# Turning the memory tokens by VectorE instead of TensorE, in a two-layer hybrid decoder kernel

## The reference, cut to what matters

```python
def rms_norm(x, g):
    return x * rsqrt(mean(x * x, axis=-1) + 1e-6) * g

mkv   = (rms_norm(mem, mem_norm_g) @ w_mem_kv).reshape(1, 256, 2, 4, 256)   # w_mem_kv: 2048 x 2048
mem_k = rms_norm(mkv[:, :, 0], mem_k_norm_g)
mem_v = mkv[:, :, 1]
h = x
h = h + even_layer(h, ..., mem_k, mem_v)  # DeltaNet, gated conv module, memory attention
h = h + odd_layer(h, ..., mem_k, mem_v)   # stick-breaking attention, memory attention
```

## Time and profile before

| what | value |
|---|---|
| median of three runs | 1333.56 us |
| the profiled execution's own time | 1333.2 us |
| its span, first to last instruction | 1331.5 us |
| VectorE busy | 972.8 us, 73% |
| ScalarE busy | 746.8 us, 56% |
| DMA queues' packets | 59% and 1% of 16 engines |
| granted TensorE clock | 1.000 |

### The profile page before, as it was taken

How to read it: one execution, slowest core, us unless ns; L and a number is a source line. 1 busy time by engine, 2 the same in 40 slices (tenths; PEclk the granted TensorE clock), 3 DMA queues, 4 the chain that set the end, 5 groups by cost and what they waited for, 6 DMA issues and landing times.

```text
span 1331.5 us, 18050 instructions
## 1 busy us (share of the span) xinstructions
PE 1324.3 (99%) x6733; PEld 1125.4 (85%) x6733; DVE 972.8 (73%) x1502; ACT 746.8 (56%) x1167; POOL 104.9 (8%) x104
## 2 busy tenths in 40 slices
PE   9999999999999999999999999999999999999998
PEld 9998899888888888888888888888888888888887
DVE  5557588898898998685656477688697787666663
ACT  6556633476435556586446446847747667764341
POOL 2000301003010100000001020020020100000000
PEclk9999999999999999999999999999999999999999
DMA  9655464555756995675455665465565565764652
GB/s 314 200 178 181 139 193 140 150 175 159 231 174 195 298 288 193 198 224 177 152 175 159 221 190 172 156 202 156 184 203 174 163 203 160 240 229 146 206 190 79
DMA packets 143153, 251.89 MB, mean 189 GB/s; under 512 B 14897, under 2 KB 27098, under 8 KB 143066
## 3 DMA queue, kind: packets, MB, share of 16 engines
q1 hardware_dynamic: 140345, 246.02, 59.0%
q10 hardware_dynamic: 2720, 4.72, 1.0%
HBM read 240.61 MB, written 10.09 MB: 188 GB/s over the span
## 4 chain that ended last, share of the span: by engine, by line
PE 79%; DVE 1%; POOL 0%; issue 0%; DVEq 0%
PE job L1820 48%; PE job L1830 24%; PE mixer L1841 2%; PE mixer L2033 1%; PE mixer L2053 1%; PE mixer L2062 1%; PE mixer L2075 1%; PE mixer L1950 0%; PE mixer L2061 0%; PE mixer L2076 0%; PE mixer L1930 0%; DVE cvr L1587 0%; DVE wlo L1339 0%; PE mixer L1963 0%; PE mixer L1938 0%
## 5 line engine op out<-in xcount | busy, mean ns | idle before, releaser
L1820 PE MATMUL job<-whi,xhi 128*128 128x512 f32 x1532 | 612.0, 399 | 0.0
L1820 PE MATMUL job<-whi,xlo 128*128 128x512 f32 x1532 | 597.5, 390 | 0.0
L1339 DVE TENSOR_TENSOR wlo<-raw,whi 128x1024 fp32r<-128x1024 f32 x431 | 524.4, 1237 | 66.7 <-ACT whi L991 65.5
L991 ACT ACTIVATE whi<-raw 128x1024 fp32r<-128x1024 f32 x431 | 445.5, 1056 | 183.5 <-PE job L1830 129.2
L1830 PE MATMUL job<-wlo,xhi 128*128 128x512 f32 x1532 | 410.1, 389 | 0.0
L1830 PEld LDWEIGHTS job<-wlo,xhi 128*128 128x128 f32 x1532 | 287.6, 188 | 60.7
L1820 PEld LDWEIGHTS job<-whi,xhi 128*128 128x128 f32 x1532 | 287.9, 188 | 57.9 <-DVE xlo L1390 0.5
L1820 PEld LDWEIGHTS job<-whi,xlo 128*128 128x128 f32 x1532 | 288.1, 188 | 57.2
L1587 DVE SCALAR_TENSOR_TENSOR cvr<-cvr,vt 128x255 f32<-128x255 f32 (+14 forms) x240 | 106.4, 502 | 0.2
L1817 PE MATMUL job<-xhi,whi 128*128 128x256 f32 x376 | 94.1, 288 | 0.0
L1817 PE MATMUL job<-xlo,whi 128*128 128x256 f32 x376 | 92.1, 283 | 0.0
(11 more groups left out here) (292 smaller groups left out, 993.2 us busy)
## 6 DMA issues: line engine op xcount, KB each, us to landing
raw<-in_od_w_in_dram SPq DMA_DIRECT2D x160, 512.0 KB, 4.4
raw<-in_ev_w_in_dram SPq DMA_DIRECT2D x143, 512.0 KB, 4.1
raw<-in_ev_w_out_dram SPq DMA_DIRECT2D x48, 512.0 KB, 5.4
raw<-in_od_w_out_dram SPq DMA_DIRECT2D x48, 512.0 KB, 5.1
raw<-in_w_mem_kv_dram SPq DMA_DIRECT2D x32, 512.0 KB, 4.9
proj<-turned_blocks SPq DMA_DIRECT2D x48, 128.0 KB, 4.4
turned_blocks<-proj SPq DMA_DIRECT2D x8, 512.0 KB, 5.4
reg<-in_mem_dram ACTq DMA_DIRECT2D x4, 512.0 KB, 5.3
```

Source lines behind the costliest of these rows:

```text
L991: act(whi[:, c % RING, :, :], raw[:, c % RAWS, :, :], ACT.Copy).then_inc(s_hi, 1)
L1339: vec.tensor_tensor(wlo[:, c % RING, :, :], raw[:, c % RAWS, :, :], whi[:, c % RING, :, :].bitcast(F32), ALU.subtract).then_inc(s_lo, 1)
L1820: mm(pj[j % 2][n][:, :], x[:, s, cols], h, start=first, stop=False)
```

## The change

`mem` is laid out so that 32 by 32 block turns, which VectorE can do, are all that is needed. Partitions 32b to 32b + 31 get the columns 512b to 512b + 511, of tokens a * 32 + j on partition 32b + j. One VectorE transpose `mt` p of 128 by 512 elements takes, of every run of 16 columns, columns 2p and 2p + 1. Its input is read with a step of 16 elements, and partition q of the result holds columns 16q + 2p and 16q + 2p + 1 for all 256 tokens: two fills. So fill 24 + k holds features k, 16 + k, 32 + k and so on, and the rows of `w_mem_kv` (2048 by 2048) are loaded in that order: partition q of chunk i of a job gets rows 16q + 2i and 16q + 2i + 1. The gains of the norm come in the same order by one small DMA more. `memt`, where the turned tiles go, has room for four fills and lies in `mix`, tiles 4 to 7. The two activations for the squares become eight of 512 columns, with sums that lie on four groups of 32 partitions; VectorE brings them together by 16 small copies and a sum. `xt` of `mem` has no TensorE step; `mt` 0 to 3 stand at positions 148, 150, 152, 154, `mt` 4 to 7 at 157, 159, 161, 163, each with .26 in the ledger.

```diff
-... "xt": .18, "mf": .16, "bas": .1}
+... "xt": .18, "mt": .26, "mf": .16, "bas": .1}
...
-        stream(5, CH0[J_MEM] - 11 + k, [(("xt", F_MEM + k), 0)])
-        stream(5, CH0[J_MEM] - 2 + k, [(("xt", F_MEM + 8 + k), 0)])
+        for half, start in ((0, CH0[J_MEM] - 11 + k), (8, CH0[J_MEM] - 2 + k)):
+            if k % 2 == 0:
+                stream(5, start - 1, [(("mt", (half + k) // 2), 0)])
+            stream(5, start, [(("xt", F_MEM + half + k), 0)])
...
-        memx = reg[:, :].rearrange("p (t d) -> p t d", t=T)
+        memx = reg[:, :].rearrange("p (a d) -> p a d", a=8)
+        memt = mflat[:, 4 * S:8 * S].rearrange("p (k s) -> p k s", k=4)
...
 def load_chunk(c):
+                if name == "mem":
+                    src = w[name][:, c0:c0 + 512].rearrange("(p k) n -> p k n", p=128)[:, 2 * (c - CH0[j]):2 * (c - CH0[j]) + 2, :]
...
+            sp.dma_start(mgain[:, :], vecs(vrow)[1][1].rearrange("k p -> (k p)").rearrange("(p k) -> p k", k=16)).then_inc(s_vrow, 16)
...
 # ScalarE, do_xt
+                if F_MEM <= n < F_OB:
+                    sc.wait_ge(s_vrow, 16 * 15)
+                    sc.wait_ge(s_jt, turn_count["mt", (n - F_MEM) // 2])
+                    fill_wait(n)
+                    act(xhi[:, SLOT[n], :], memt[:, n % 4, :], ACT.Copy, scale=xt_gain(n)).then_inc(s_xh, 1)
+                    return
...
 # ScalarE, do_rstd
+                if src == 1:
+                    for a in range(8):
+                        ins = act(pflat[:, 512 * (a % 4):512 * (a % 4) + 512], memx[:, a, :], ACT.Square, accum_out=msum[:, a:a + 1])
+                        if a == 3:
+                            link(ins)
...
 # ScalarE, do_mload
-                sc.dma_start(memx[:, :, 512 * b:512 * b + 512],
-                             mem[:, 512 * b:512 * b + 512].rearrange("(t p) d -> p t d", p=128)).then_inc(s_min, 16)
+                sc.dma_start(memx[32 * b:32 * b + 32], mem[:, 512 * b:512 * b + 512].rearrange("(a j) d -> j a d", j=32)
+                             ).then_inc(s_min, 16)
...
 # VectorE
+            def do_mt(p):
+                ve.wait_ge(s_min, 64)
+                ve.wait_ge(s_xl, F_OA + 8 if p < 2 else F_MEM + 2 * p - 2)
+                vec.transpose(memt[:, 2 * (p % 2):2 * (p % 2) + 2, :].rearrange("p k s -> p (k s)"),
+                              memx.rearrange("p a (i k) -> p k a i", k=16)[:, 2 * p:2 * p + 2]).then_inc(s_jt, 1)
...
 # VectorE, do_xt
+                    vec.scalar_tensor_tensor(out=xlo[:, SLOT[n], :], in0=memt[:, n % 4, :], scalar=xt_gain(n),
+                                             in1=xhi[:, SLOT[n], :].bitcast(F32), op0=ALU.mult, op1=ALU.subtract).then_inc(s_xl, 1)
...
 # VectorE, do_rstd
+                if src == 1:
+                    for a in range(4):
+                        for b in range(4):
+                            ins = vec.tensor_copy(mquar[32 * a:32 * a + 32, :, b], msum[32 * b:32 * b + 32, a:8:4])
+                    link(ins)
+                    link(vec.tensor_reduce(ssq[:, src, :], mquar[:, :, :], AX.X, ALU.add))
...
 # TensorE, do_xt
+                if F_MEM <= n < F_OB:
+                    return
```

More of the change, by code:

```diff
@@ L461, in prog, with blocks_turned @@
         tanhs = {0: slot(2), 1: slot(3), 4: tiles(20), 5: tiles(0), 10: slot(0), 11: slot(1)}
+        turn_no = {i: n for n, i in enumerate(i for st, i in plan if st == "lt")}
+        turn_count = {q: n + 1 for n, q in enumerate(q for q in plan if q[0] in ("lt", "mt"))}
         def exchanged(e, transfers=5):
-            return s_xg[e % 3], 80 * (e // 3) + 16 * transfers
+            return s_xg[turn_no[e] % 3], 80 * (turn_no[e] // 3) + 16 * transfers
+        def blocks_turned(e):
+            return s_jt, turn_count["lt", e]
         def landed(e):
@@ L635, in banks @@
             if step == "xt":
-                return [i % 3 if 8 <= i < F_OB else i % 4]
+                return [] if F_MEM <= i < F_OB else [i % 3 if 8 <= i < F_OA else i % 4]
             if step == "mao":
@@ L721, in xt_gain @@
         def xt_gain(n):
-            return (gain("ev_norm_g", n) if n < F_OA else gain("mem_norm_g", n - F_MEM) if n < F_OB
+            return (gain("ev_norm_g", n) if n < F_OA else mgain[:, n - F_MEM:n - F_MEM + 1] if n < F_OB
                     else gain("od_norm_g", n - F_H))
         def turned(n):
-            return n + 1 if n < F_OA else n - F_MEM + 17 if n < F_OB else n - F_H + 33
+            return n + 1 if n < F_OA else n - F_H + 17
         def mix_tile(n):
@@ L773, in load_chunk @@
                     sp.wait_ge(s_lo, c - RAWS + 1)
-                sp.dma_start(raw[:, c % RAWS, :, :], w[name][r:r + 256, c0:c0 + 512].rearrange("(k p) n -> p k n", p=128)
-                             ).then_inc(s_raw[c % RAWS], 16)
+                if name == "mem":
+                    src = w[name][:, c0:c0 + 512].rearrange("(p k) n -> p k n", p=128)[:, 2 * (c - CH0[j]):2 * (c - CH0[j]) + 2, :]
+                else:
+                    src = w[name][r:r + 256, c0:c0 + 512].rearrange("(k p) n -> p k n", p=128)
+                sp.dma_start(raw[:, c % RAWS, :, :], src).then_inc(s_raw[c % RAWS], 16)
             sp.dma_start(*vecs(vrow)[0]).then_inc(s_gain, 16)
@@ L823, in do_xw @@
             def do_xw(e):
[L824 to L827, removed]
+                sp.wait_ge(*blocks_turned(e))
+                if turn_no[e] >= 3:
+                    sp.wait_ge(s_xg[turn_no[e] % 3], 80 * (turn_no[e] // 3))
+                sp.dma_start(bass.AP(dram_x, 131072 * e, [[1024, 128], [1, 1024]]), stage[e]).then_inc(s_xg[turn_no[e] % 3], 16)
             def do_xr(e):
@@ L1049, in do_rstd @@
                     sc.wait_ge(s_scp, 4)
-                o = 0 if src == 1 else 2048
-                link(act(pflat[:, 0:2048], (memx if src == 1 else hid)[:, 0, :], ACT.Square, accum_out=ssq[:, src, 0:1]))
-                ins = act(pflat[:, o:o + 2048], (memx if src == 1 else hid)[:, 1, :], ACT.Square, accum_out=ssq[:, src, 1:2])
+                if src == 1:
[3 more added lines that the diff above has]
+                            link(ins)
+                    ins.then_inc(s_ss, 1)
+                    return
+                o = 2048
+                link(act(pflat[:, 0:2048], hid[:, 0, :], ACT.Square, accum_out=ssq[:, src, 0:1]))
+                ins = act(pflat[:, o:o + 2048], hid[:, 1, :], ACT.Square, accum_out=ssq[:, src, 1:2])
                 ins.then_inc(s_ss, 1)
@@ L1666, in do_lt @@
                     ve.wait_ge(s_mks, e - 5)
-                    ve.wait_ge(*((s_z, 16) if e == 6 else (s_xl, F_OA + 8)))
+                    ve.wait_ge(*((s_z, 16) if e == 6 else (s_xl, F_OB)))
                 elif e in (9, 10):
```

15 lines of the change are left out of this document (8 added, 7 removed).

## The result

The changed kernel takes 1340.93 us (median of 4 runs, 1338.13 to 1341.14) against 1333.22 of the kernel before on the same chip. The profiled execution took 1341.14, its span 1339.4.

A forecast was written before the change was run, and what follows sets the result against it. TensorE, busy 99%, was taken to bound the kernel: 4.1 us of transposes removed, less waits of 1.45 and 1.7 us (3.1 together), net -1.0, from 1333.56 to 1332.6 us; range 1329.3 to 1336.8.

The forecast's parts named there:

- TensorE's 0.256 us per pair: Each fill's pair of `mem` transposes costs TensorE this much; removing 16 pairs gains 4.1 us.
- both waits: New TensorE waits for VectorE's `xlo` at chunk 167, 1.45 us, and GpSimd's `lnacc` at 169, 1.7 us.
- The ledger's order: Eight entries of .26 move conv items later: item 123 from position 163 to 167, `lnm` from 165 to 169.
- VectorE's wait for the squares: At `rstd`, VectorE waits 4.4 us for ScalarE's eight squares, not 3.09 as before.
- The `w_mem_kv` loads at nothing: Weight loads whose neighbouring partitions read 128 KB apart, not 8 KB, were taken to cost nothing.
- The block turn: Each `mt` on VectorE takes 0.62 us from start to start, from a turn of as many elements at 0.71.
- The row nearest to it: Trace row with a 64-byte step on the writing side, 15 elements, 163 ns; taken as support for 0.62 us.
- the second rival: Strided read makes each block turn nearly twice as long: 3.2 us more, net +2.2, 1335.8 us; chance 0.17.
- The copies: 16 small copies on VectorE at `rstd`: 1.1 to 2.7 us, 1.2 taken.
- GpSimd's sums: GpSimd's two sums after conv item 123 take 2.60 us, making `lnacc` ready at 547.0.
- The second wait: TensorE, already delayed by 1.45 us, waits 1.7 us more for GpSimd's `lnacc` at `lnm`, ahead of chunk 169.
- 43 us of cover: Last `mem` load, issued at 440.24, is first needed at 488.75; no plausible landing exceeds that.

The follow-up runs named there:

- the version with both waits moved and the plain read: Changed kernel with the row sums at position 168, `lnm` at 170 and block turns reading 512 neighbouring elements: 1330.45 us, ratio 0.9977.
- the two profiles: Profiles of the changed kernel in its first measurement (1340.93 us) and when run again without edit (1339.04 us, ratio 1.0044).
- the 128-partition form: Changed kernel with the same layout of `mem`, loaded by eight DMAs of 128 partitions by 512 columns instead of four of 32 partitions: 1355.49 us.
- the plain-read version: Changed kernel with its eight block turns of `mem` reading 512 neighbouring elements instead of every 16th: 1337.63 us, ratio 1.0038.

## Why the prediction was wrong

**Right.** TensorE's 0.256 us per pair, as the steps between 149 and 160 show, and whole in the version with both waits moved and the plain read. The ledger's order: item 123 and `lnm` where it put them. The place and the owner of both waits, `xlo` at 167 and `lnacc` at 169. VectorE's wait for the squares, 4.4 forecast, 4.18 measured. The `w_mem_kv` loads at nothing. (TensorE's waits before are six, in five groups, not five; nothing hangs on it.)

**The block turn, 0.62 taken, 0.98 measured from start to start.** The row nearest to it, on writes of 15 elements, was no evidence on a read of 512: 15 elements at 0.7 ns more are 10 ns, too little to be seen in it. The six turns that the forecast counted are 2.2 us. It let turns 0 and 1 vanish in the wait before `zg` 5, but there is no such wait: VectorE comes to `zg` 5 without a pause, at 501.80 and 498.27 in the two profiles, so all eight count, 2.9 us. Taking the step out gives 3.2 us of the stage between the two profiles without a wait at 146 (5.4 to 2.2), and 1.4 or 3.3 of the medians. This was the second rival. Its place and sign were right, its price above the measured one (1.15), and its sum below the time, for the steps that follow.

**The copies, 1.2 taken, 2.8 measured.** They were priced by 128-partition operations at 0.07. These cross partition groups, and come each 0.17, the upper bound that the text gave. Within their groups they took 1.5. In medians it is worth 0.7 us, with intervals as wide.

**GpSimd's sums, 2.60 taken, 4.5 to 4.8 measured.** With the clock behind it, this step alone turns the sign: with VectorE's two prices as forecast the kernel is still 3.8 us slower. VectorE's prices alone would have turned it too: 2.2 and 1.6 us more in the forecast's sum make 1336.4. The 2.60 was measured beside a VectorE with gaps. The forecast filled the gaps, and kept the number. The second wait, 1.7 in the forecast, is 3.6 in the three profiles where TensorE came to it at the full clock, and 1.6 where the lower clock at 167 had held TensorE back already. That VectorE's work beside it is the cause rests on where the sums end, 0.6 us behind the last `rest` of an unbroken run in eleven profiles, behind an `xlo` from SBUF in a twelfth, and on their lengths (0.73 for one alone; for both 1.8 beside an `xlo` and a block turn, 2.5 to 2.6 beside one `rest`, 4.5 to 4.8 beside `rest` back to back), not on a run that changes this alone. The Trainium skill's page "GPSIMD Engine Reference", section "1. Specifications", has GpSimd share its SBUF interfaces with VectorE and contend with instructions of two SBUF inputs, which `rest` is; it gives no size. The rows agree.

**The clock, not in the sum.** Behind a new wait TensorE ran some 3.4 us at 1.2 GHz, about 1.7 us lost: twice in the changed kernel's first profile, once in its second. The forecast let a wait cost its own length; at 2.4 GHz it costs 0.3 more, and with the lower clock some 2 more.

**The wait at 160, not looked for.** The forecast held VectorE against chunks 167 and 169 only. VectorE's backlog shows first at the `evac` behind the copies, where TensorE waits 0.6 and 1.5 us. In the end this adds nothing, since VectorE runs without a pause from the copies to its last conv item, and TensorE waits for that: what it loses at 160 it doesn't lose later.

**The wait at 146, not in the sum.** 2.0 us and the clock's 1.6, in the first profile and not in the second. I gave the `mem` loads 43 us of cover and asked only whether they come in time for their own user. They did. They may have been late for somebody else, an exchange in a stage whose DMA share is 0.95. What is shown is the slower landing, the longer write where the wait came, and more slow executions of the kernel before with these loads. That the loads lengthen the write isn't shown: with the same loads it took 8.0 to 9.6 us in seven profiles, moving them made it worse, and the 128-partition form did not work. The cause of this wait stays open.

**The sum, closed for both profiles.** First: -4.1 of transposes, +0.7 before the stage, +3.6 at 146, +0.9 at 160 (wait 0.6), +4.2 at 167 and 168 (2.3 and the clock), +1.9 at 169: +7.2, against +7.27 at the last chunk. Second: -4.1, +0.2 before the stage, -0.3 at 146, +1.8 at 160 (wait 1.5), +2.7 at 167, +5.5 at 169 (3.6 and the clock): +5.8, against +5.59.

The second can be closed along the forecast's own steps too. It had `lnacc` ready at 547.0, and it was ready at 551.7. 2.2 of these 4.7 us are GpSimd's. 2.5 are VectorE's: the copies and the sum behind them 1.5, and the four turns that follow 1.4, less 0.4, since the squares ended that much sooner. TensorE then pays 0.3 to start again and 1.6 for the clock. -1.0 and 6.6 make +5.6.

**What the chances missed.** The rivals changed one price each. The waits are in series on one VectorE, so errors of one sign add: the turns 2.2, the copies 1.6, GpSimd 2.2, the clock 1.6. Both of VectorE's prices at the bounds that the text gave, 3.2 and 1.5 us over those taken, make 1332.6 + 4.7 = 1337.3, outside the range as given.

## What to carry to other kernels

Work moved from the engine that bounds the kernel to one 86% busy is paid where the second engine waits for something else: move such a wait behind the next deadline (here the row sums, worth 7 to 9 us), and give the new work its entry in the scheduler's ledger. A duration measured beside idle neighbours isn't the duration once you fill them; ask of each row what ran beside it. And ask of a load not only whether it is early enough for its own user, but what else travels beside it: here that question was left out, and part of the loss stayed unexplained.

## What the runs showed of the hardware

- A VectorE block turn of 128x512 takes 703 ns from neighbouring elements and 1064 ns at a read step of 64 bytes (the plain-read version, the changed kernel).
- Sixteen 32x2 copies take 2.8 us when they cross partition groups, 1.5 within them. One lasts 0.15 to 0.16 us in both cases; only those within a group overlap.
- A GpSimd addition of 128x256 takes 0.73 us alone and up to 3.9 beside VectorE's subtractions back to back; it ends 0.6 us after the last of them. VectorE pays too: sixteen copies beside two such additions took 3.8 us instead of 2.8.
- The granted clock fell to 1.2 GHz in or behind twelve TensorE waits of 2.04 to 9.5 us, in the changed kernel for 3.4 us each time, and not behind two of 2.29 and 2.34, nor those of 1.6. What else decides it stays open.
- At 2.4 GHz a TensorE wait of 0.84 us cost 1.12, one of 1.58 cost 1.86.
- Loads of 512 KB into 32 partitions landed in 7.6 to 9.9 us, where the same bytes over 128 took 5.3.
